# Modulation tiles in front of the units of a q/k/v projection, and the split of the next weight tile behind a unit's second sum

## The reference, cut to what matters

```python
mod_lat = (silu_c @ w_ada[i] + b_ada[i])[:, None, :]
mod_ctx = silu_cc @ w_ada[i] + b_ada[i]
sh_a, sc_a, g_a, sh_m, sc_m, g_m = jnp.split(mod_lat, 6, axis=-1)
h_lat = x * (1.0 + sc_a) + sh_a
h_ctx = xc * (1.0 + csc_a) + csh_a
q, k, v = jnp.split(h @ w_qkv, [1024, 1280], axis=-1)
q = rms_norm(q.reshape(b, n, 16, 64), q_norm)
k = rms_norm(k.reshape(b, n, 4, 64), k_norm)
if rotate: q, k = apply_grid_rope(q, rope), apply_grid_rope(k, rope)
```

## Time and profile before

| | |
|---|---|
| runs | 2874.57, 2874.82, 2875.98 us (median 2874.82) |
| the profiled execution | 2874.26 us |
| its span in the trace | 2872.5 us |
| PE busy | 2607.8 us (91%) |
| VectorE, ScalarE, POOL busy | 1445.7, 1041.1, 743.6 us |
| HBM read | 252.62 MB |

### The profile page before, as it was taken

How to read it: one execution, slowest core, us unless ns; L and a number is a source line. 1 busy time by engine, 2 the same in 40 slices (tenths; PEclk the granted TensorE clock), 3 DMA queues, 4 the chain that set the end, 5 groups by cost and what they waited for, 6 DMA issues and landing times.

```text
span 2872.5 us, 39059 instructions
## 1 busy us (share of the span) xinstructions
PE 2607.8 (91%) x16373; PEld 1442.9 (50%) x16584; DVE 1445.7 (50%) x2179; ACT 1041.1 (36%) x1713; POOL 743.6 (26%) x985
## 2 busy tenths in 40 slices
PE   4789999889999998889999999887898998899997
PEld 1346665645556576357654445544543333344443
DVE  2336884773342125688664422665765653433322
ACT  2335773333231113567543322322342213422221
POOL 1220000248787722400040000033253543011100
PEclk7899999999999999999999999999989999999998
DMA  6220003345552221210035532221112323233321
GB/s 222 103 88 16 2 2 118 115 160 189 197 176 84 93 75 49 67 59 2 30 118 186 189 109 90 78 96 52 52 52 73 99 70 110 59 103 103 99 96 55
DMA packets 206078, 268.26 MB, mean 93 GB/s; under 512 B 8975, under 2 KB 188558, under 8 KB 196686
## 3 DMA queue, kind: packets, MB, share of 16 engines
q1 hardware_dynamic: 199758, 243.97, 26.5%
q0 software_dynamic: 5280, 18.64, 1.8%
q10 hardware_dynamic: 864, 3.15, 0.3%
HBM read 252.62 MB, written 10.49 MB: 92 GB/s over the span
## 4 chain that ended last, share of the span: by engine, by line
PE 69%; DVE 16%; ACT 5%; issue 3%; POOL 3%; DMA 3%; SPq 0%; POOLq 0%; DVEq 0%; ACTq 0%
PE PS L289 19%; PE PS L288 19%; PE PS L290 19%; DVE WB L284 2%; PE PS L487 2%; PE PS L851 2%; DVE SM L933 2%; DVE AR L939 2%; ACT WB L274 1%; DMA WS<-in_mlp_w 1%; DMA WS<-in_gqa_w_qkv 1%; DVE X L1216 1%; DVE GT L1225 1%; PE PS L632 1%; PE PS L1999 1%
## 5 line engine op out<-in xcount | busy, mean ns | idle before, releaser
L289 PE MATMUL PS<-H,WB 128*128 128x512 bf16 (+1 forms) x1953 | 686.2, 351 | 30.5 <-DVE WB L284 10.5
L288 PE MATMUL PS<-H,WB 128*128 128x512 bf16 (+2 forms) x1907 | 668.2, 350 | 25.5 <-DVE WB L284 13.7
L290 PE MATMUL PS<-H,WB 128*128 128x512 bf16 (+2 forms) x1949 | 683.5, 351 | 1.2
L284 DVE TENSOR_TENSOR WB<-WS,WB 128x2048 bf16<-128x2048 f32 (+3 forms) x165 | 375.5, 2276 | 583.4 <-ACT WB L274 583.3
L274 ACT ACTIVATE WB<-WS 128x2048 bf16<-128x2048 f32 (+3 forms) x165 | 295.5, 1792 | 663.5 <-PE PS L290 424.9
L288 PE MATMUL PS<-AR,WB 128*128 128x512 bf16 (+1 forms) x1279 | 431.6, 337 | 15.8 <-DVE WB L284 7.6
L289 PE MATMUL PS<-AR,WB 128*128 128x512 bf16 (+1 forms) x1280 | 431.7, 337 | 8.1 <-DVE AR L1615 4.8
L290 PE MATMUL PS<-AR,WB 128*128 128x512 bf16 (+1 forms) x1281 | 431.7, 337 | 1.1
L288 PEld LDWEIGHTS PS<-H,WB 128*128 128x128 bf16 x1976 | 194.4, 98 | 298.5 <-issue 65.2
L290 PEld LDWEIGHTS PS<-H,WB 128*128 128x128 bf16 x1976 | 195.2, 99 | 176.4 <-issue 9.2
L289 PEld LDWEIGHTS PS<-H,WB 128*128 128x128 bf16 x1976 | 194.9, 99 | 165.5 <-issue 7.7
(11 more groups left out here) (399 smaller groups left out, 3781.3 us busy)
## 6 DMA issues: line engine op xcount, KB each, us to landing
WS<-in_mlp_w SPq DMA_DIRECT2D x64, 1024.0 KB, 5.6
WS<-in_w_ada SPq DMA_DIRECT2D x48, 1024.0 KB, 5.0
WS<-in_w_in SPq DMA_DIRECT2D x26, 1024.0 KB, 5.1
WS<-in_ada_w SPq DMA_DIRECT2D x24, 1024.0 KB, 4.9
WS<-in_ffn_w_in SPq DMA_DIRECT2D x44, 512.0 KB, 4.8
e_scratch<-EB POOLq DMA_DIRECT2D x16, 512.0 KB, 3.7
EB<-e_scratch POOLq DMA_DIRECT2D x16, 512.0 KB, 3.6
WS<-in_ffn_w_out SPq DMA_DIRECT2D x8, 1024.0 KB, 5.4
```

Source lines behind the costliest of these rows:

```text
L284: e.tensor_tensor(lo, staged(i), hi, SUB).then_inc(dv.sem, dv.mark(("lo", i)))
L288: e.matmul(out_, l[0], r[0], start=start, stop=False)
L289: e.matmul(out_, l[0], r[1], start=False, stop=False)
L290: return e.matmul(out_, l[1], r[0], start=False, stop=stop)
```

## The change

`sums` gets a hook `front`, called at each unit's first tile, once PE has waited for that tile's lower half and before its first sum. In the q/k/v stage it issues modulation tiles 8 and 9 in front of unit one, 10 and 11 in front of unit two, 12 and 13 in front of unit three, and 14 and 15 in front of unit four; unit zero has none. The entry `BESIDE["qkv"]` goes. The order of tiles becomes: unit 0, unit 1, t8, t9, unit 2, t10, t11, unit 3, t12, t13, unit 4, t14, t15, v. ScalarE and VectorE split the next weight tile only in the iterations u = 1, 5, 9, 13 and 17 (a unit's second sum), behind the square and behind the gain, no longer in front of them at u = 0, 4, 8, 12 and 16. The copy of set 1 now stands in front of the square of u = 16, its turn behind sum 16 on PE (behind `swap(14)` and `head(15)`), and the bias behind the gain of 16. No instruction is added or taken away; the line numbers shift by a few.

```diff
--- before.py
+++ after.py
@@ -296,7 +296,8 @@
         def groups(units, segs):
             return [(i, key, s) for i, (_, _, ms) in enumerate(units) for key, _, _ in ms for s in segs]
 
-        def sums(e, tag, src, units, nks, rhs, segs, then=None, whole=False, ring="dense", first=0):
+        def sums(e, tag, src, units, nks, rhs, segs, then=None, whole=False, ring="dense", first=0, front=None):
+
 
             for i, (c0, nc_, ms) in enumerate(units):
                 if i < first:
@@ -304,6 +305,8 @@
                 banks, k0, kt = {}, 0, sum(nks)
                 for c, nk in enumerate(nks):
                     w, hi, lo = tile(e, (tag, i, c), src[k0 * 128:(k0 + nk) * 128, c0:c0 + nc_], nk, nc_, whole)
+                    if front and c == 0:
+                        front(e, i)
                     for key, off, M in ms:
                         for s in segs:
                             if k0 == 0:
@@ -526,8 +529,7 @@
 
 
 
-        BESIDE = {"qkv": ([("ada0", t) for t in range(8, 16)], 2, 4, "side5"),
-                  "wo0": ([("ada0", t) for t in range(16, 24)], 2, 4, "side5"),
+        BESIDE = {"wo0": ([("ada0", t) for t in range(16, 24)], 2, 4, "side5"),
                   ("w1", 0): ([("ada1", t) for t in range(24)] + [("ada2", t) for t in range(8)], 2, 4, "side"),
                   ("w1", 1): ([("ada2", t) for t in range(8, 24)], 1, 2, "side")}
 
@@ -644,9 +646,15 @@
                     swap(u - 2)
                 if u > 0:
                     head(u - 1)
-                beside_pe(e, "qkv", u)
-
-            linear(e, "qkv", a["gqa_w_qkv"][0], QKV, [8], h_of("in"), (0, 1), then, ring="five")
+                if u == 16:
+                    ada_turn_pe(e, "ada0", 1, "side5")
+
+            def front(e, i):
+
+                for t in range(6 + 2 * i, 8 + 2 * i) if i else ():
+                    ada_pe(e, "ada0", t, "side5")
+
+            linear(e, "qkv", a["gqa_w_qkv"][0], QKV, [8], h_of("in"), (0, 1), then, ring="five", front=front)
             w, hi, lo = tile(e, ("v", 0, 0), a["gqa_w_qkv"][0][:, 1280:1536], 8, 256)
             for j in range(6):
                 b = bank(e, "five", ("v", j))
@@ -678,12 +686,14 @@
             def first(u):
                 key, s = QU[u]
                 raw, sq, n = qkv_bufs(u)
-                high_halves(e, next_tiles("qkv", key // 2))
+                if u == 16:
+                    ada_act(e, "ada0", 1)
                 pe.wait_ge(e, ("qkv", key, s))
                 if u > 5:
                     dv.wait_ge(e, ("turned", u - 6))
                 e.activation(sq, ps(bank_of["qkv", key, s], n), SQUARE).then_inc(ac.sem, ac.mark(("sq", u)))
-                beside_act(e, "qkv", u)
+                if u % 4 == 1:
+                    high_halves(e, next_tiles("qkv", key // 2))
 
             def second(u):
                 raw, sq, n = qkv_bufs(u)
@@ -713,13 +723,15 @@
             def first(u):
                 key, s = QU[u]
                 raw, sq, n = qkv_bufs(u)
-                low_halves(e, next_tiles("qkv", key // 2))
                 if u > 5:
                     old = QU[u - 6][0]
                     (po if old < 8 else dv).wait_ge(e, ("q" if old < 8 else "k", u - 6))
                 ac.wait_ge(e, ("sq", u))
                 e.tensor_scalar(raw, ps(bank_of["qkv", key, s], n), qg if key < 8 else kg, 0.125 if key < 8 else 1.0, MUL, MUL).then_inc(dv.sem, dv.mark(("raw", u), ("free", ("qkv", key, s))))
-                beside_dve(e, "qkv", u)
+                if u % 4 == 1:
+                    low_halves(e, next_tiles("qkv", key // 2))
+                if u == 16:
+                    ada_dve(e, "ada0", 1)
 
             def second(u):
                 raw, sq, n = qkv_bufs(u)
```

## The result

| | before | changed |
|---|---|---|
| runs | 2873.93 to 2875.98, median 2874.7 us (4) | 2857.56 to 2859.39, median 2858.28 us (4) |
| profiled execution | 2874.26 us | 2859.39 us |
| span | 2872.5 us | 2857.6 us |
| first sum of the stage to the head at v | 151.7 us | 134.9 us |
| behind that head | 2660.7 us | 2661.4 us |

The ratio is 0.9945, 95% interval 0.9932 to 0.9959: 16.4 us faster by the medians. The prediction was 2858.4. The stage is 16.8 us shorter. (The first matmul of the stage has no record in the first two traces; I put its start 0.43 us, one matmul at 1.2 GHz, before the first recorded one.)

The account below looks back on a forecast made before the run. PE, with 69% of the chain that ended last, was taken as the bound; 17.7 + 2.0 - 2.0 - 1.3 = 16.4 us off 2874.82 gave 2858.4, range 2856.5 to 2860.5 (eight in ten: 2855 to 2865).

Parts of the forecast that it names:

- Units one to three: PE's six pairs there: 91.57 us become six of 11.32 plus three fronts of 2.0, together 73.9; 17.7 us removed.
- Unit zero: First unit of q/k/v: head's 1.00 us wait and low-clock tile of 1.70 us go; 2.0 us gained, between 1.5 and 3.6.
- the reading nearest to the row: In unit zero, the clock rises when it did before, some 2.4 us of sums at half speed: 1.5 us gained.
- Unit four: Last unit: new front costs 2.0 us; PE's 3.8 us wait for ScalarE's copy, with the low clock, loses 1.3 more.
- the row of the 2.93 us wait: Old profile's wait in unit four, taken as the low clock's price: 1.1 in sum, 0.35 in head, 0.1 at issue, 1.6 us.
- The second tile: Rival: each front's second tile lands late, four waits up to 2.1 us, 2866.8 at worst; chance 0.12. Forecast: 1.4 us to spare.
- the slower rival: Between head sums of units one to four PE's clock stays low, about 10 us more a pair, up to 2938; chance 0.03.
- the term for the shared port: VectorE and GpSimd locking each other out, up to 2.3 us per rotation if the split slid onto it; left out.
- best of both bounds: Rival: clock rises early in unit zero and stays up in unit four; 19.6 us gained, 2855.2; chance 0.10.
- nothing behind swallowed it: Rival: a later load or VectorE stage absorbs the gain, time between 2858 and 2875; chance 0.05.

Follow-up runs that it names:

- e4: Kernel before with the split behind a unit's second sum, modulation tiles in the middles of both pairs, turn behind sum sixteen; 2845.12 us, ratio 0.99.
- e4_again: The kernel of e4 run a second time without an edit; 2845.5 us, ratio 0.9897 to the kernel before.
- e3: Changed kernel with the turn of the modulation sums and its bias one sum later, behind sum seventeen; 2852.05 us, ratio 0.9922 to the kernel before.
- e2: Changed kernel with both splits back in front of the square of a unit's first sum, fronts kept; 2873.68 us, ratio 0.9997 to the kernel before.
- e5: Changed kernel with both splits one sum later, behind a unit's third sum; 2893.47 us, ratio 1.0065 to the kernel before.
- e7: The kernel of e2 run a second time without an edit; 2871.37 us, ratio 0.9985 to the kernel before.

## Why the prediction was right, point by point

**Units one to three: right.** Six pairs and three fronts: 73.9 predicted, 165.32 - 91.55 = 73.77 measured, 17.8 us removed for 17.7. The plain pair was 11.32 to the hundredth; a front cost 1.95 for 2.0. That the tile in a pair's middle had been covering the ordinary wait, which the prediction named as the reason why a front costs its full price, is shown by e4: 11.32 with the tile in it, and 11.32 in the changed kernel without.

**Unit zero: mechanism right, gain under-sized.** 2.0 predicted. From the first sum to the head at its second pair it is 30.29 us after and 33.24 before, 2.95 gained. The clock was the term: in the changed kernel's timeline two matmuls of the same kind near the start of the second pair, at 81.29 and 81.96, are three matmuls or 0.67 us apart, full speed, so next to nothing of that sum ran low, where the prediction let 2.4 us run low:

```profile
79.16 1.91 PE L634 MATMUL PS<-AR,KM 128*128 128x512 f32 x2
81.29 0.40 PE L289 MATMUL PS<-H,WB 128*128 128x512 bf16 x1 [0.22 <-issue]
...
81.96 0.38 PE L289 MATMUL PS<-H,WB 128*128 128x512 bf16 x1
```

So the reading nearest to the row was the wrong end here. Why the clock rose earlier is not shown: it was granted at 0.50 from about 76 to 82 us before and from about 78 to 81 after, and with one and the same code e4_spread ran the head of sum zero at full speed (1.02 us) and e4_again at the low clock (1.91).

**Unit four: mechanism right, loss under-sized.** From head fourteen to the rotation product of sixteen: 20.92 before (205.80 - 184.88), 24.86 after. That is 3.9 us lost where 3.3 were predicted (2.0 for the front and 1.3 for the rest). The wait was 3.65 for 3.8, at the place and for the reason given. Mis-sized was the low clock behind it, 1.6 by the row of the 2.93 us wait: the turn lost 0.5 us and sum seventeen 2.1, 2.6 together. e3 took this wait away and 4.5 us went.

The sum: 17.8 + 2.95 - 3.9 = 16.8 in the stage, against 16.4. The two mis-sized terms have opposite signs and sizes of 0.95 and 0.6, so the agreement of the total to a tenth of a microsecond is luck; that of units one to three is not.

**The rivals.** The second tile landed in time. In front two it is loaded at 111.7, lands 4.9 us later, at 116.6, and PE wants it at 118.1, 1.5 us to spare for the 1.4 predicted; in the four fronts it took 4.9 to 5.0 us, and no L490 waited. The clock stayed up through the ordinary waits, granted at 1.00 from 91.5 to 174 us, so the slower rival's mechanism did not occur. The Trainium skill (TensorE: Matmul & The Clock Gate, on oscillation) tells of a wait that recurs between bursts and throttles each burst anew; the DMA waits in its example are longer, 3 to 5 us. This trace shows nothing of the kind at waits of 1.13 us. POOL worked beside neither of the first two moved splits (84.56 to 86.85 and 109.41 to 111.70; POOL's next products start at 87.45 and 112.04), and its 256-column product took 0.67 us in the pairs around them, so the term for the shared port was rightly left out. Of the best of both bounds one half came: unit zero's 2.95 lies nearer to its 3.6 than to 1.5, but the clock fell in unit four. The argument against it there, that waits of 2.93 us and more all lowered the clock, holds for the one trace it was read from and not for e2, e5 and e7 (last section). And the end shows the stage's gain, so nothing behind swallowed it.

**What the prediction did not ask** is which of the two edits earns the gain. It costed them together. The runs show that the split's move alone earns 26 us of stage, and that the tile order adds a cost of 9.5 back: fronts where nothing is covered (2.5 in units one to three, 1.95 in unit four), and the turn put where PE must stand for it, 5.5, less 0.45 from the emptied unit zero.

## What to carry to other kernels

When an engine waits in its queue for a load in front of something that another engine needs, try to move the waiting instruction behind it before touching the order of loads; here that alone beat the larger change by some 10 us. It must not slip so far that the next user waits: one sum later the kernel was 19 us slower than before the change. Filler work belongs where the bounding engine waits anyway: the same tile cost 0.98 us in front of a unit (half of 1.95) and nothing in the middle of a pair. And a small step on the bounding engine that reads another engine's result must be placed by that engine's queue order, not by when its own input is done: the turn stood 3.65 us for a copy whose input, the last tile's product, had been whole since about 168.3 us.

## What the runs showed of the hardware that was not expected

A wait of one and the same length did not cost the same each time. The three waits of 2.93 us in e2 were followed by heads of 1.65, 2.05 and 1.10 us. Windows over the first and the third wait and the stretch behind each (columns as in the earlier trace rows) show the granted clock, 0.57 once and 1.00 the other time, though both waits were equally idle:

```profile
105.20:108.06 2.86, 0.00 (x0) 1.00 0.00 0
108.06:111.00 2.94, 2.94 (x6) 0.57 0.26 42
161.20:164.05 2.85, 0.00 (x0) 1.00 0.00 0
164.05:167.00 2.95, 2.95 (x12) 1.00 0.25 36
```

e7 is the same code. There the first wait cost nothing, and behind the third the clock stayed low for most of the next sum, so that it is 9.07 us from that head to the rotation product where it is 6.12 at full speed, 2.95 us lost; in e2 it was the other way round, 7.81 and 6.11:

```profile
105.77 1.10 PE L634 MATMUL PS<-AR,KM 128*128 128x512 f32 x2 [2.92 <-ACT AR L695]
...
160.16 2.05 PE L634 MATMUL PS<-AR,KM 128*128 128x512 f32 x2 [2.93 <-ACT AR L695]
...
169.23 1.02 PE L641 MATMUL PS<-AR,KM 128*128 128x512 f32 x2
```

The turn's wait of 3.65 us, which cost the changed kernel 2.6 us more at the low clock, cost nothing of the kind in e5, where the turn ran in 0.66 us and the sum behind it at full speed:

```profile
211.90 0.66 PE L505 MATMUL PS<-KM,STAT 128*128 128x128 f32 x4 [3.65 <-ACT STAT L499]
...
215.02 1.02 PE L634 MATMUL PS<-AR,KM 128*128 128x512 f32 x2
```

So the price of a wait near 3 to 4 us is the wait itself plus anything from nothing to 3 us, and it differs between two executions of the same code. Both mis-sized terms of the prediction depend on when the clock falls and rises; such a term deserves a range and not a row's value. The cause of the difference was not tested.
